# HGRN values mixed and turned ahead of the retention values, output quarters in another order, the last half projected by tokens

## The reference, cut to what matters

```python
h = h + hybrid_mixer(rms_norm(h, norm1_g[layer]), w_in[layer], ...)
h = h + expert_choice_ffn(rms_norm(h, norm2_g[layer]), w_router[layer], w_gate[layer], w_up[layer], w_down[layer])

def hybrid_mixer(...):     # 4 retention heads and 4 HGRN heads of 128 columns
    ...
    r_out = from_heads(rms_normalize(r_out)) * ret_g * jax.nn.silu(rg)   # norm per head
    h_out = rms_norm(from_heads(h_out), hgrn_g) * jax.nn.silu(hg)        # norm over 512 columns
    return jnp.concatenate([r_out, h_out], axis=-1) @ w_out              # [1024, 1024]

def expert_choice_ffn(...):  # 16 experts, each takes its 32 best tokens
    affinity = jax.nn.softmax(xn @ w_router, axis=-1)
    gate, idx = lax.top_k(jnp.swapaxes(affinity, 1, 2), cap)
    ...   # per expert three matrices of 1024 x 1024: w_gate, w_up, w_down
```

## Time and profile before

| what | value |
|---|---|
| median of 3 runs | 1857.3 us (1857.11 to 1859.0) |
| the profiled execution | 1856.24 us, of which span 1854.4 us |
| PE busy | 1454.0 us, 78% |
| DVE, ACT, POOL busy | 799.2, 571.2, 62.2 us |
| DMA | 563.14 MB, mean 304 GB/s |

### The profile page before, as it was taken

One profiled execution on the slowest core, in us unless ns is written; L12 is line 12 of the kernel. 1 busy time (PEld: TensorE's weight loads), 2 busy tenths in 40 slices (PEclk: granted clock), 3 DMA queues, 4 the chain that ended last, 5 costly groups with the idle time before them and its releaser, 6 DMA issues.

```text
span 1854.4 us, 24842 instructions
## 1 busy us (share of the span) xinstructions
PE 1454.0 (78%) x10541; PEld 1069.3 (58%) x10541; DVE 799.2 (43%) x1246; ACT 571.2 (31%) x898; POOL 62.2 (3%) x56
## 2 busy tenths in 40 slices
PE   8999999999999999985555445579999555555546
PEld 7999999989999898861212112149886121111212
DVE  5767777776777799830101001019973010000101
ACT  4655555465554585321000000028532100000001
POOL 1010000010000000100000000002010000000000
PEclk9999999999999999998777778789999877777868
DMA  9426555534655385799999999997479999999997
GB/s 325 145 70 226 191 174 173 171 104 154 199 182 182 110 271 161 294 372 430 429 430 430 430 429 429 430 394 245 153 293 369 430 429 429 430 430 429 430 429 315
DMA packets 165492, 563.14 MB, mean 304 GB/s; under 512 B 12600, under 2 KB 116534, under 8 KB 137606
## 3 DMA queue, kind: packets, MB, share of 16 engines
q1 hardware_dynamic: 155318, 551.49, 76.2%
q10 hardware_dynamic: 10064, 10.06, 1.8%
HBM read 558.05 MB, written 1.05 MB: 301 GB/s over the span
## 4 chain that ended last, share of the span: by engine, by line
PE 54%; issue 23%; DMA 17%; DVE 3%; ACT 2%; POOL 1%; SPq 0%; POOLq 0%; PEldq 0%; ACTq 0%; DVEq 0%
PE psum L2682 6%; PE psum L2721 5%; PE psum L2976 5%; PE psum L2659 5%; PE psum L2661 5%; PE psum L2660 5%; DMA ring<-in_w_down 5%; DMA ring<-in_w_up 3%; DMA arena<-in_w_gate 3%; PE psum L2711 3%; PE psum L2831 2%; PE psum L2958 2%; PE psum L2576 2%; DMA arena<-in_w_down 2%; DMA arena<-in_w_up 2%
## 5 line engine op out<-in xcount | busy, mean ns | idle before, releaser
L2976 PE MATMUL psum<-ring,arena 128*32 128x512 f32 (+1 forms) x1600 | 280.6, 691 | 198.4 <-DMA ring<-in_w_down 77.8
L2976 PE MATMUL psum<-arena 128*32 128x512 f32 x1024 | 207.6, 702 | 149.5 <-DMA ring<-in_w_up 40.3
L2976 PEld LDWEIGHTS psum<-ring,arena 128*32 128x32 f32 x1600 | 70.7, 128 | 346.0 <-issue 343.4
L907 DVE TENSOR_TENSOR W<-ring,W 128x2048 fp32r<-128x2048 f32 (+1 forms) x92 | 206.3, 2243 | 85.1 <-ACT W L888 84.5
L2274 DVE TENSOR_TENSOR arena<-arena,psum 128x512 f32<-128x512 f32 x16 | 11.0, 690 | 452.7 <-PE psum L2976 452.7
L2659 PE MATMUL psum<-XT,W 128*128 128x256 f32 x704 | 199.4, 283 | 0.0
L2661 PE MATMUL psum<-XT,W 128*128 128x256 f32 x704 | 199.1, 283 | 0.0
L2660 PE MATMUL psum<-XT,W 128*128 128x256 f32 x704 | 199.0, 283 | 0.0
L888 ACT ACTIVATE W<-ring 128x2048 fp32r<-128x2048 f32 (+1 forms) x92 | 172.3, 1872 | 78.7 <-PE psum L2661 42.5
L2976 PEld LDWEIGHTS psum<-arena 128*32 128x32 f32 x1024 | 50.5, 127 | 251.4 <-issue 251.4
L2660 PEld LDWEIGHTS psum<-XT,W 128*128 128x128 f32 x704 | 134.9, 192 | 0.9
(11 more groups left out here) (341 smaller groups left out, 2619.0 us busy)
## 6 DMA issues: line engine op xcount, KB each, us to landing
ring<-in_w_down SPq DMA_DIRECT2D x36, 2048.0 KB, 30.0
ring<-in_w_up SPq DMA_DIRECT2D x32, 2048.0 KB, 31.2
ring<-in_w_up SPq DMA_DIRECT2D x58, 1024.0 KB, 5.1
ring<-in_w_gate SPq DMA_DIRECT2D x28, 2048.0 KB, 33.5
ring<-in_w_in SPq DMA_DIRECT2D x54, 1024.0 KB, 7.6
arena<-in_w_up SPq DMA_DIRECT2D x24, 2048.0 KB, 32.9
arena<-in_w_down SPq DMA_DIRECT2D x20, 2048.0 KB, 29.9
arena<-in_w_gate SPq DMA_DIRECT2D x20, 2048.0 KB, 29.8
```

The lines of the kernel that those rows point to most:

```text
L907: nc.vector.tensor_tensor(W2[split_pair(v)][:, c], slot(v % SLOTS_1)[:, c], W1[split_pair(v)][:, c].bitcast(F32), ALU.subtract).then_inc(r ...
L2976: last = nc.tensor.matmul(psum[CAP * e:CAP * (e + 1), b, 0:cols.stop - cols.start], src[:, 4 * half + k, CAP * e:CAP * (e + 1)], tiles[e][ ...
```

## The change

Five things, in both layers of the second block:

1. PE makes the HGRN values right behind the last input projection, then the scores, then turns the HGRN half, and only then makes the retention values. ACT and DVE are reordered to match; the decays of heads 2 and 3 stand behind the HGRN outputs on DVE.
2. The products of the output projection go 0, 1, 2, 4, 5, 6, 3, 7. P7 is made for the first 128 tokens, then for the other 128, in two banks, and what follows it (adding to X, turning, logits) is split by tokens in the same way. Inside a product the two matmuls that read the ring slot's rest stand earlier.
3. A slot of `w_out` is given back by the last but one matmul of its product, not by `release`. The last slots of the input projection are given back behind the first head's scores; before it was behind the fourth's.
4. SP: home 6 waits for P3, homes 5 and 7 and XT for all of the output projection (`wo_mm` 5, before 2, 4 and the logits); all three homes now stand behind n = 19. n = 22 and 23 are loaded in two halves of 0.5 MB each, and a half's place is given back after half of the first quad.
5. POOL no longer multiplies the router weights with -1; DVE makes one small instruction less between logits and exponential, and the last of four one-hot instructions stands behind the first gathered rows.

```diff
-OUT_HOMES = {5: (18, 2), 6: (19, 4), 7: (19, 4)}
+OUT_HOMES = {6: (19, None), 5: (19, 5), 7: (19, 5)}
+OUT_BUFFER = [0, 1, 2, 3, 0, 1, 2, 0]
+OUT_ORDER = [0, 1, 2, 4, 5, 6, 3, 7]
+OUT_BANK = [(4, 4), (5, 5), (6, 6), (7, 5)]
+RAW_BANK = [(0, 0), (1, 1), (2, 2), (3, 6)]
+BY_HALF_SLOTS = (22, 23)
...
+                def half_slot(s, src, j):
+
+                    sp.wait_ge(slot_free[s], j + 1)
+                    if j == 1:
+                        sp.sem_clear(slot_free[s])
+                    sp.dma_start(slot(s)[:, j * D:(j + 1) * D], src[:, j, :]).then_inc(slot_loaded[s], 16)
...
-                        sp.wait_ge(logits, past(logits) + 1)
+                        sp.wait_ge(wo_mm, past(wo_mm) + 5)
...
-                                    sp.wait_ge(wo_mm, past(wo_mm) + OUT_HOMES[home][1])
+                                    if OUT_HOMES[home][1]:
+                                        sp.wait_ge(wo_mm, past(wo_mm) + OUT_HOMES[home][1])
+                                    else:
+                                        sp.wait_ge(proj2, past(proj2) + len(ITEMS) + 4)
...
+                    elif n == 7:
+                        act.wait_ge(wo_mm, past(wo_mm) + 1)
...
-                for n in range(4):
-                    round_out(n)
+                round_out(0)
...
+                for n in range(1, 4):
+                    round_out(n)
+                turn_mixer_act(act, past, 1, 3)
...
-                for n in range(4, 8):
+                for n in OUT_ORDER[3:]:
                     rest_of_out(n)
...
-                turn_raw_dve(3)
+                turn_raw_dve(2)
+
+                def add_last(t):
+
+                    dve.wait_ge(wo_mm, past(wo_mm) + 3 + t + 1)
+                    dst = X[:, t, 768:1024]
+                    nc.vector.tensor_tensor(dst, psum[:, OUT_BANK[3][t], t * S:(t + 1) * S], dst, ALU.add).then_inc(x_mid, 1)
+
+                add_last(0)
+                turn_raw_dve(3, 0)
+                add_last(1)
+                turn_raw_dve(3, 1)
...
+                for h in range(HEADS):
+                    item(ITEM_AT["score", h])
+                    if h == 0:
+                        release(None, 0, [])
...
+                pe.wait_ge(mix_done, past(mix_done) + TT)
+                for nth, b in ((0, 2), (1, 3)):
+                    turn_half(nth, b)
                 pe.wait_ge(emp_dve, past(emp_dve) + SPLIT_FROM + HEADS)
...
+                        if n == 7 and t == 1 and k == 2:
+                            turn_raw(3, 0)
+                        for m, (x, wt) in enumerate(((mixed_first, w1), (mixed_first, w2), (mixed_rest, w1))):
...
+                            if (t, k, m) == (TT - 1, 3, 1):
+                                last.then_inc(slot_free[mixer_slot(lay, N_IN2 + i)], 1)
...
-                for i in range(4):
-                    project_half(4 + i).then_inc(wo_mm, 1)
-                    release(wo_mm, past(wo_mm) + i + 1, [mixer_slot(lay, N_IN2 + i)])
+                both_tokens(2).then_inc(proj2, 1)
+                for i in range(3):
+                    both_tokens(4 + i).then_inc(wo_mm, 1)
                     if i:
                         turn_raw(i - 1)
-                    if i >= 2:
-                        raw_logits(i - 2)
-                release(None, 0, [])
-                turn_raw(3)
+                raw_logits(0)
+                both_tokens(3).then_inc(proj2, 1)
+                turn_raw(2)
+                raw_logits(1)
+                project_half(7, 0).then_inc(wo_mm, 1)
                 raw_logits(2)
-                raw_logits(3).then_inc(logits, 1)
+                project_half(7, 1).then_inc(wo_mm, 1)
+                raw_logits(3, 0)
+                turn_raw(3, 1)
+                raw_logits(3, 1).then_inc(logits, 1)
...
-                                if k == 1 and cols.stop == D and homes[e][1] is None:
+                                if cols.stop == D and homes[e][1] is None and (k == 1 or (g, mat, pair) == (0, 0, 0) and e < 2):
                                     last.then_inc(slot_free[homes[e][0]], 1)
```

More of the change, by code:

```diff
@@ L2155, in _, with decayed_scores @@
                         normalise_first_rows(BY_ROWS[:2])
-                dve.wait_ge(decay_in, 16 * (lay + 1))
-                for h in range(HEADS):
+                def decayed_scores(h):
                     n = ITEM_AT["score", h]
@@ L2795, in _ @@
                 item(ITEM_AT["in", 17])
-                for h in range(HEADS):
-                    item(ITEM_AT["score", h])
-                release(None, 0, [])
                 pe.wait_ge(merged, past(merged) + LEVELS)
@@ L2806, in _, with turn_half @@
                     last.then_inc(h_mixed, 1)
+                for h in range(HEADS):
+                    item(ITEM_AT["score", h])
+                    if h == 0:
+                        release(None, 0, [])
+                def turn_half(nth, b):
+                    for i in range(2):
+                        for t in range(TT):
+                            last = nc.tensor.transpose(psum[:, nth, (2 * i + t) * P:(2 * i + t + 1) * P],
+                                                       XN[:, t, (2 * b + i) * P:(2 * b + i + 1) * P], ident)
+                    last.then_inc(turned, 1)
+                pe.wait_ge(mix_done, past(mix_done) + TT)
+                for nth, b in ((0, 2), (1, 3)):
+                    turn_half(nth, b)
                 pe.wait_ge(emp_dve, past(emp_dve) + SPLIT_FROM + HEADS)
@@ L2813, in _, with project_half @@
                     last.then_inc(r_mixed, 1)
-                def turn_half(nth, b):
-                    for i in range(2):
-                        for t in range(TT):
-                            last = nc.tensor.transpose(psum[:, nth, (2 * i + t) * P:(2 * i + t + 1) * P],
-                                                       XN[:, t, (2 * b + i) * P:(2 * b + i + 1) * P], ident)
-                    last.then_inc(turned, 1)
-                def project_half(n):
+                def project_half(n, t):
@@ L2849, in raw_logits @@
                         for k in (2 * i, 2 * i + 1):
[L2850 to L2855 removed]
+                            last = nc.tensor.matmul(psum[:, 4, u * EXPERTS:(u + 1) * EXPERTS], raw_turned[:, k, u * P:(u + 1) * P], wr[:, k, :],
+                                                    start=(u == k == 0), stop=(k == KD - 1), skip_group_check=True)
@@ L2940, in single_quad @@
                         if g == 0:
-                            for home in homes:
-                                loaded(home)
+                            for e, home in enumerate(homes):
+                                loaded(home, 1 + ((mat * PAIRS + pair) * GROUP + e in BY_HALF_SLOTS))
                         elif last_quad:
```

134 lines of the change are left out of this document (72 added, 62 removed).

## The result

The changed kernel takes **1862.84 us** (median of 9 runs, 1861.54 to 1864.93), the kernel before 1857.28 us (9 runs): ratio 1.0031, 95% interval 1.0023 to 1.0040. That is 5.6 us slower. The forecast was 1858.3, a change of 1 us that a measurement would not tell from none. The value is inside the range (1851 to 1863), but the kernel is measurably slower.

What follows compares the result with a forecast made beforehand. The DMA stream of expert weights, full at 430 GB/s, was taken to bound the kernel. Each layer's stream ends 0.4 us later, 0.5 with thin transfers: 1856.24 + 1 = 1857.2, median 1.1 above, so 1858.3; range 1851 to 1863.

Steps and rivals of the forecast that it cites:

- What bounds the kernel, and that PE counts only by what it releases: Experts' stretches: DMA is full at 429 to 430 GB/s, PE's work is covered; only holes before the stream settles count.
- Start of the chain, +0.4 at P0: Mixer, ahead of the output projection: PE idles about 1 us and 0.7 us, so P0 starts 0.4 us later.
- Stalls inside the products: Output projection: waits of 0.2 us at P4 and 0.45 us at X's first turn; products end at 1408.0.
- Behind P7: From the last product to the experts: logits at about 1410.4, first quad near 1419.7, +2.2 us on PE.
- The stream: "Then the halves of n = 22 and 23 ... +0.4": Weight stream ahead of the experts: first halves issued at 1421.6 against 1421.19, so each layer's stream ends 0.4 us later.
- I charge 0.1: Loading n = 22 and 23 as four thin transfers was to cost 0.1 us a layer.
- The prediction's own sign: Test of being wrong: 24th piece's data end not within 1.5 us of 1428.4, or the stretch behind not full.
- The one on the halves: Halves at n = 22 and 23 cost a lone transfer each time, 2.5 us a layer: 1863.3; chance 0.10.
- The homes are too late: Output projection ends too late, so its issue of homes decides; 1.6 us a layer, 1861.5; chance 0.08.
- PE is not later: PE's waits mostly covered, quad near 1417.5, stream ends 3 us earlier a layer: 1851.5; chance 0.22.
- nothing moves: Holes in the stream shift but their sum stays: within 1 us of 1857.3, inside the forecast's own range.

Runs made afterwards that it cites:

- b_late: Kernel before with 8 idle products (about 2.2 us) on PE ahead of each layer's first gathered rows; 1862.11 us, ratio 1.0028.
- b_values: Kernel before with part 1 of the change alone; 1859.24 us, ratio 1.0013.
- b_slack: Kernel before with part 1 alone, but P2 made ahead of the second turns and the rests of P3 and P4 earlier on DVE; 1856.83 us, ratio 0.9996.
- a_warm: Changed kernel with more idle products on PE, 7 for 5 and 16 for 13, between logits and first quad; 1861.45 us, ratio 1.0026.
- a_wholewarm: Changed kernel with n = 22 and 23 loaded whole and with 7 and 16 idle products; 1860.93 us, ratio 1.0020.
- b_thin: Kernel before with n = 22 and 23 in halves, all four given free together after the whole first quad; 1859.31 us, ratio 1.0010.
- b_homes: Kernel before with home 5 issued behind n = 19 and P7, like homes 6 and 7; 1858.84 us, ratio 1.0011.
- a_tail: Changed kernel with part 2 and the homes of part 4 undone, the halves kept; 1860.70 us, ratio 1.0017.

## Why the prediction was wrong

1. *What bounds the kernel, and that PE counts only by what it releases*: right. b_late puts a number to it, one us a layer for each us of the first quad, and the 20 layers with n = 22 whole agree within 0.4 us.
2. *Start of the chain, +0.4 at P0*: did not occur; P0 begins at +13.0 in both. The two waits ahead of it were there, but 0.65 and 0.23 us, not 1 and 0.7.
3. *Stalls inside the products*: 0.2 and 0.45 were charged, for P4 and for the turn of X's first quarter; the first came about so, the second was 0.18. The wait behind P1, 0.6 us, was not seen; b_values and b_slack show it. The errors partly cancel: the products' end was forecast at +42.0 (1408.0) and is +42.45 (1411.06 + 0.73 in the chain above, less T0), the logits at +44.4 and are at +44.5. a_warm's first quad, at a steady clock, is +54.0 for a forecast of +53.7.
4. *Behind P7*: right at a steady clock. The fall of the clock between logits and quad was not foreseen. In the profiled execution of the changed kernel it makes the quads 1.2 and 0.9 us later and the layers 1.1 and 1.8 us longer than a_warm's.
5. *The stream: "Then the halves of n = 22 and 23 ... +0.4"*, with "I charge 0.1". **This is the step that failed**: the term for the halves was 0.1 us a layer and measured 1.6. A quad that is 2.2 us later was to cost 0.5, because the halves are issued half a quad, 1.85 us, earlier. In a_warm, without a fall of the clock, the quads are 2.5 us later and the first halves are issued at +55.9 (forecast +55.6), 0.7 us later than n = 22 was before; this part was nearly right. But the last half lands at +65.5 and +65.9, where n = 23 landed at +62.7 and +62.6 before and the forecast was 0.4 later than that. The layers are 2.3 us longer in place of 0.5, 1.6 us more than the later issue accounts for (by the seventh doubles, before the layer's end, 0.8 and 1.3). a_wholewarm, without halves, is as slow. So the halves cost what they are issued earlier, and a quad that is 2.5 us later costs nearly all of it. The four thin transfers were not as good as two whole ones once the queue had drained; which part of it is SP's four issues and which the transfers' is open. The prediction's own sign agrees: the 24th piece's data were to end within 1.5 us of 1428.4, 0.4 later than before, and in the changed kernel the piece landed at +66.4, 3.8 us later than before.
6. *Rivals.* The one on the halves had nearly the right time (1863.3) and part of the right cause, but at 2.5 us a layer it was too dear (1.6), and its condition, a stream at rest between first and second halves, did not occur: the stream ran on, at 262 GB/s in the us shown, and b_thin loses without any wait between them. That its 1863.3 lies near 1862.8 is in part luck, since the clock's falls are in the latter. "The homes are too late" did not decide in the changed kernel (homes 5 and 7 from +42.5 on, forecast +42.1), though b_homes shows a way in which late homes cost, by n = 7, that I had not priced. "PE is not later" was excluded by the quads (+55.2 and +54.9, before +51.5), and "nothing moves" by the time.

The 5.6 us by runs: part 1 alone is +2.4 (b_values), the changed kernel without part 2 and the homes +3.1 (a_tail), with them +5.6; a_tail's and after's intervals touch. In the profiled executions the difference is 7.5 us: 2.3 us a layer at a steady clock, and 1.1 and 1.8 more for the falls, which the profiled execution of before doesn't have. The clock is in each of the medians too, and with intervals of 1.6 us its share can't be separated in the medians. What decides whether an execution has the fall stays open.

## What to carry to other kernels

Before moving work ahead of a serial step, ask what that work's results were covering: part 1 gave the HGRN chain its cover by taking the retention chain's, and one product more between (b_slack) settles it. When a stream runs dry at one late issue, holes ahead of that issue are free and filling them gains nothing; the event that releases it counts, as long as no piece ahead of it comes so late that its user waits (b_homes). Splitting a transfer to release it earlier shortens nothing by itself: here 1.85 us of earlier issue were lost again before the last half had landed. Price such a split by the last landing, not by the first issue.

## What the hardware showed that I had not expected

- In a drained queue the first 1 MB piece landed 4.9 to 5.3 us after its issue (22 layers; a lone 1 MB 4.9) and the first 0.5 MB piece after 3.8 to 4.4, once 5.6. The same 2 MB took 7.4 to 7.7 us in two pieces, 8.2 and 9.2 in four that were released together, and 9.2 to 10.6 in four that were released in pairs.
- The granted clock fell from 1.00 to 0.50 for about 3.4 us in PE's work between logits and first quad, in some executions and layers and not in others of the same kernel. In the changed kernel's two layers it fell behind waits of 0.52, 0.60 and 1.01 us among idle products, but a_tail and b_slack had it right behind the logits, after work that was nearly without a gap, the last of it the logits' 128x16 matmuls. The Trainium skill, "TensorE: Matmul & The Clock Gate", What's actually happening, gives the same two levels, 1.2 and 2.4 GHz, and ties the lower one to an idle array; these rows agree on the levels, and in a_tail and b_slack not on the cause.
